# Two layers of block 1: turned dilated heads, weight parts and out weights in another order

## The reference

```python
h = rmsnorm(x, attn_norm[l])
c_q, c_kv, k_r, q_d, k_d, v_d = jnp.split(h @ w_in[l], split_at, axis=-1)
o_a = mla_mixer(c_q, c_kv, k_r, cos, sin, g_cq[l], g_ckv[l], w_uq[l], w_ukv[l], ...)
q_d = rmsnorm(q_d.reshape(B, S, DIL_HEADS, DIL_HD), g_dil_q[l])
k_d = rmsnorm(k_d.reshape(B, S, DIL_HEADS, DIL_HD), g_dil_k[l])
o_b = dilated_attention(q_d, k_d, v_d, rel_bias)
mixed = jnp.concatenate([o_a.reshape(B, S, -1), o_b.reshape(B, S, -1)], axis=-1)
x = x + mixed @ w_out[l]
x = x + conv_ffn(rmsnorm(x, ffn_norm[l]), w_up[l], conv_w[l], conv_b[l], w_down[l])
```

## Time and profile before

| | us |
|---|---|
| median of 3 runs | 1795.7 (1791.6 to 1797.75) |
| profiled execution | 1792.91 |
| its span, first to last instruction | 1791.1 |
| PE busy | 1646.6 |
| DVE busy | 1128.8 |
| ACT busy | 844.1 |
| POOL busy | 263.7 |
| mean granted clock of TensorE | 0.972 |

### The profile page before, as it was taken

How to read it: one execution, slowest core, us unless ns; L and a number is a source line. 1 busy time by engine, 2 the same in 40 slices (tenths; PEclk the granted TensorE clock), 3 DMA queues, 4 the chain that set the end, 5 groups by cost and what they waited for, 6 DMA issues and landing times. The chain is left out here.

```text
span 1791.1 us, 22878 instructions
## 1 busy us (share of the span) xinstructions
PE 1646.6 (92%) x8652; PEld 1323.4 (74%) x8652; DVE 1128.8 (63%) x1881; ACT 844.1 (47%) x1506; POOL 263.7 (15%) x322
## 2 busy tenths in 40 slices
PE   8989999998999999798799899999999696989996
PEld 7667887785687877586557688888787584668875
DVE  5586898466768995625574744444333656579964
ACT  5554776364646664522153633333222532466643
POOL 2000114500021118000000001111630000001171
PEclk9999999999999999999999999999999798989998
DMA  7456765554678545431264533333222341236651
GB/s 258 151 204 178 204 191 172 193 174 151 214 241 215 162 151 186 139 102 47 74 229 122 160 99 94 94 94 96 93 94 95 118 136 47 70 108 188 188 188 47
DMA packets 266496, 258.32 MB, mean 144 GB/s; under 512 B 8822, under 2 KB 208730, under 8 KB 266131
## 3 DMA queue, kind: packets, MB, share of 16 engines
q1 hardware_dynamic: 262706, 245.36, 45.0%
q0 software_dynamic: 3536, 11.42, 1.8%
q10 hardware_dynamic: 144, 0.07, 0.0%
HBM read 255.72 MB, written 1.10 MB: 143 GB/s over the span
## 5 line engine op out<-in xcount | busy, mean ns | idle before, releaser
L551 PE MATMUL psv<-hHL,wH 128*128 128x512 f32 (+1 forms) x1952 | 639.6, 390 | 12.4 <-issue 9.0
L1167 DVE TENSOR_TENSOR wL<-ring,wH 128x1024 fp32r<-128x1024 f32 (+2 forms) x364 | 451.8, 1247 | 296.3 <-ACT wH L1715 293.3
L1715 ACT ACTIVATE wH<-ring 128x1024 fp32r<-128x1024 f32 (+2 forms) x364 | 376.2, 1040 | 311.3 <-PE psv L551 305.4
L551 PE MATMUL psv<-hHL,wL 128*128 128x256 f32 (+1 forms) x1504 | 466.7, 310 | 0.0
L551 PEld LDWEIGHTS psv<-hHL,wH 128*128 128x128 f32 x1952 | 365.0, 189 | 94.9 <-issue 10.5
L551 PE MATMUL psv<-wH,hHL 128*128 128x512 f32 (+2 forms) x936 | 321.3, 392 | 39.7 <-DVE wL L1167 27.5
L551 PEld LDWEIGHTS psv<-hHL,wL 128*128 128x128 f32 x1504 | 285.3, 190 | 15.9
L551 PE MATMUL pss<-wH,hHL 128*128 128x512 f32 (+3 forms) x808 | 274.9, 385 | 0.0
L551 PEld LDWEIGHTS psv<-wH,hHL 128*128 128x128 f32 x936 | 177.2, 190 | 84.6 <-DVE wL L1167 22.6
L551 PE MATMUL psv<-wL,hHL 128*128 128x512 f32 (+2 forms) x468 | 181.4, 388 | 0.0
L551 PEld LDWEIGHTS pss<-wH,hHL 128*128 128x128 f32 x808 | 153.1, 191 | 29.7
(11 more groups left out here) (238 smaller groups left out, 1758.9 us busy)
## 6 DMA issues: line engine op xcount, KB each, us to landing
ring<-in_w_up SPq DMA_DIRECT2D x176, 512.0 KB, 5.2
ring<-in_w_mod SPq DMA_DIRECT2D x96, 512.0 KB, 4.8
ring<-in_w_down SPq DMA_DIRECT2D x88, 512.0 KB, 4.4
ring<-in_w_in SPq DMA_DIRECT2D x52, 512.0 KB, 4.7
ring<-in_w_out SPq DMA_DIRECT2D x32, 512.0 KB, 4.7
ring<-in_w_in SPq DMA_DIRECT2D x8, 384.0 KB, 5.9
ring<-in_w_in SPq DMA_DIRECT2D x8, 288.0 KB, 6.8
ring<-in_w_ukv SPq DMA_DIRECT2D x4, 512.0 KB, 4.3
```

The lines of the kernel that those rows point to most:

```text
L551: return pe.matmul(o, a, b, start=start, stop=stop, skip_group_check=True)
L1167: v.tensor_tensor(lo, raw, hi.bitcast(F32), ALU.subtract).then_inc(piece_split, told("piece_split", p))
L1715: return ac.activation(o, i, ACT.Copy)
```

## The change

- In part 2 of the input projection ACT converts the next weight piece (2.2) before the latent squares instead of behind them, and the roots of the four sums are taken together at the end, two columns at a time (`squares` in place of `sumsq`).
- PE turns the dilated heads behind the lifts, ahead of the bands and of part 4, instead of behind part 4. DVE's and ACT's copies of them move ahead too, DVE's before the sums of the lifted heads, ACT's behind their squares. The squares of the first token tile go to another area of `W`.
- ACT converts piece 4.2 between the lift copies; DVE makes its low part before its copies of the turned heads (4.0 and 4.1 stay where they were). ACT no longer waits for `dil_heads`, and loads the table of the exponential before it copies the dilated values.
- Pieces out 0.0 and out 0.1 are no longer split before the attention: ACT takes out 0.0 in step 8 and out 0.1 behind the attention, DVE takes out 0.0 in step 8 and out 0.1 in step 9, each ahead of that step's other work.
- All modulation chunks of the attention come before the out weights in the order of the chunks.

```diff
-        sqm = [w_at(14464, 16, MQK), view(scr, 0, 16, MQK)]
+        sqm = [w_at(10368, 16, MQK), view(scr, 0, 16, MQK)]
...
-            add_cols(A["w_out"][l], 0, 512, ph, "out", 0, between=lambda: add_mod(0, MOD1[l]["pairs"].values()))
+            add_mod(0, MOD1[l]["pairs"].values())
+            add_cols(A["w_out"][l], 0, 512, ph, "out", 0)
...
+                pe.wait_ge(dil_heads, at("dil_heads", ph))
+                for t in range(NT):
+                    for g in range(2):
+                        transposes("VS"[g], (ph, "dT", t, g),
...
                 if l == 0:
                     pe.wait_ge(table_spread, at("table_spread", "all"))
...
                 project_split(range(NT), [512] * NT, (ph, "in", 4))
-                pe.wait_ge(dil_heads, at("dil_heads", ph))
-                for t in range(NT):
-                    for g in range(2):
-                        transposes("VS"[g], (ph, "dT", t, g),
...
+            def attention(ph, units, l=0, mods={}, heads=None, early=(0, ())):
...
+                    if p in early[1]:
+                        splits_to(early[0], p - early[1][0])
...
+                splits_to(first_piece[ph, "in", 4], 2)
+                for t in range(NT):
+                    v.wait_ge(V_full, at("V_full", ph, "dT", t, 0))
+                    b = bank("V", ph, "dT", t, 0)
+                    v.tensor_scalar(dT[:, 0:4, t * P:(t + 1) * P], b[:, :].rearrange("p (k n) -> p k n", k=4),
+                                         col("g_dil_q", l), None, ALU.mult).then_inc(V_free, told("V_free", ph, "dT", t, 0))
                 for t in range(NT):
                     v.wait_ge(head_squares, at("head_squares", ph, "mla", t))
...
-                splits_to(first_piece[ph, "in", 4], 2)
                 v.wait_ge(head_roots, at("head_roots", ph, "mla"))
...
-                input_rows(4, dvh[:, 0, :, :])
-                for t in range(NT):
-                    v.wait_ge(V_full, at("V_full", ph, "dT", t, 0))
...
-                splits_to(first_piece[ph, "out", 0], 1)
+                v.wait_ge(V_full, at("V_full", ph, "in", 4, 0))
+                v.tensor_copy(dvh[:, 0, :, :], bank("V", ph, "in", 4, 0)[:, :].rearrange("p (h d) -> p h d", h=8)).then_inc(V_free, told("V_free", ph, "in", 4, 0))
...
-                attention(ph, units1, 0, MOD1[l]["pairs"], mla_columns)
+                attention(ph, units1, 0, MOD1[l]["pairs"], mla_columns, (first_piece[ph, "out", 0], (8, 9)))
...
+            def squares(x, n, c, *key):
+
+                ac.wait_ge(sum_of_squares, at("sum_of_squares", *squared[-1]))
+                squared.append(key)
+                ac.activation(junk[:, 0:n], x, ACT.Square, accum_out=ss[:, c:c + 1]).then_inc(sum_of_squares, mark("sum_of_squares", *key))
+                ac.wait_ge(sum_of_squares, at("sum_of_squares", *key))
...
+                splits_to(first_piece[ph, "in", 2])
                 for base, off, n in ((0, 0, QL), (3, QL, KVL)):
                     for t in range(NT):
                         ac.wait_ge(FREE["VS"[t]], at("VS"[t] + "_free", ph, "in", 1 if base else 0, t))
-                        sumsq(lat[:, t, off:off + n], n, 8 + (2 if base else 0) + t, ph, "lat", base, t)
+                        squares(lat[:, t, off:off + n], n, 8 + (2 if base else 0) + t, ph, "lat", base, t)
+                for f, o in ((ACT.Sqrt, root), (ACT.Identity, ss)):
+                    for c, n in ((8, QL), (10, KVL)):
+                        ins = ac.activation(o[:, c:c + 2], ss[:, c:c + 2], f, scale=1.0 / n, bias=eps_col[:, 0:1])
+                ins.then_inc(root_ready, mark("root_ready", ph, "lat", 3, 1))
...
+                splits_to(first_piece[ph, "in", 4], 2)
                 for c in range(2):
                     for t in range(NT):
                         ac.wait_ge(S_full, at("S_full", ph, "lift", 3, c, t))
...
-                ac.wait_ge(dil_heads, at("dil_heads", ph))
...
+                for t in range(NT):
+                    ac.wait_ge(S_full, at("S_full", ph, "dT", t, 1))
+                    b = bank("S", ph, "dT", t, 1)
+                    copy(dT[:, 4:8, t * P:(t + 1) * P], b[:, :].rearrange("p (k n) -> p k n", k=4), col("g_dil_k", l)).then_inc(S_free, mark("S_free", ph, "dT", t, 1))
...
-                input_rows(4, dvh[:, 1, :, :])
...
-                splits_to(first_piece[ph, "out", 0], 1)
+                splits_to(first_piece[ph, "in", 4] + 3, 0)
+                load_table(ACT.Exp)
+                ac.wait_ge(S_full, at("S_full", ph, "in", 4, 1))
+                copy(dvh[:, 1, :, :], bank("S", ph, "in", 4, 1)[:, :].rearrange("p (h d) -> p h d", h=8)).then_inc(S_free, mark("S_free", ph, "in", 4, 1))
...
-                attention(ph, units1, mla_columns)
+                attention(ph, units1, mla_columns, (first_piece[ph, "out", 0], (8,)))
```

More of the change, by code:

```diff
@@ L862, in _ @@
                         owed.append(used)
+                pe.wait_ge(dil_heads, at("dil_heads", ph))
+                for t in range(NT):
+                    for g in range(2):
+                        transposes("VS"[g], (ph, "dT", t, g),
+                                   [(dqk[:, t, 8 * g + 2 * k:8 * g + 2 * k + 2, :].rearrange("p a b -> p (a b)"),
+                                     slice(k * P, k * P + P)) for k in range(4)])
                 if l == 0:
@@ L869, in _ @@
                 project_split(range(NT), [512] * NT, (ph, "in", 4))
-                pe.wait_ge(dil_heads, at("dil_heads", ph))
-                for t in range(NT):
-                    for g in range(2):
-                        transposes("VS"[g], (ph, "dT", t, g),
-                                   [(dqk[:, t, 8 * g + 2 * k:8 * g + 2 * k + 2, :].rearrange("p a b -> p (a b)"),
-                                     slice(k * P, k * P + P)) for k in range(4)])
                 def mla_transposes(t):
@@ L1241, in low_features1 @@
                                         ALU.subtract).then_inc(FREE[kind], told(kind + "_free", ph, "hT", t))
-            def attention(ph, units, l=0, mods={}, heads=None):
+            def attention(ph, units, l=0, mods={}, heads=None, early=(0, ())):
                 n = len(units) // 2
@@ L1519, in _ @@
                 rotate(x1, x2, tab, tmp).then_inc(mla_heads, told("mla_heads", ph))
-                input_rows(4, dvh[:, 0, :, :])
-                for t in range(NT):
-                    v.wait_ge(V_full, at("V_full", ph, "dT", t, 0))
-                    b = bank("V", ph, "dT", t, 0)
-                    v.tensor_scalar(dT[:, 0:4, t * P:(t + 1) * P], b[:, :].rearrange("p (k n) -> p k n", k=4),
-                                         col("g_dil_q", l), None, ALU.mult).then_inc(V_free, told("V_free", ph, "dT", t, 0))
-                splits_to(first_piece[ph, "out", 0], 1)
+                v.wait_ge(V_full, at("V_full", ph, "in", 4, 0))
+                v.tensor_copy(dvh[:, 0, :, :], bank("V", ph, "in", 4, 0)[:, :].rearrange("p (h d) -> p h d", h=8)).then_inc(V_free, told("V_free", ph, "in", 4, 0))
                 def mla_columns(t):
@@ L1798, in to_features, with attention @@
                     copy(hH[:, :, t * P:(t + 1) * P], raw_h[:, t % 2, :, :]).then_inc(feat_high, mark("feat_high", ph, t))
-            def attention(ph, units, heads=None):
+            def attention(ph, units, heads=None, early=(0, ())):
                 n = len(units) // 2
@@ L1953, in _ @@
                 head_root(*(a[:, 32:64].rearrange("p (t h) -> p t h", t=NT) for a in (hroot, hx)), MQK, 8, ph, "mla")
-                input_rows(4, dvh[:, 1, :, :])
-                for t in range(NT):
-                    ac.wait_ge(S_full, at("S_full", ph, "dT", t, 1))
-                    b = bank("S", ph, "dT", t, 1)
-                    copy(dT[:, 4:8, t * P:(t + 1) * P], b[:, :].rearrange("p (k n) -> p k n", k=4), col("g_dil_k", l)).then_inc(S_free, mark("S_free", ph, "dT", t, 1))
-                splits_to(first_piece[ph, "out", 0], 1)
+                splits_to(first_piece[ph, "in", 4] + 3, 0)
+                load_table(ACT.Exp)
+                ac.wait_ge(S_full, at("S_full", ph, "in", 4, 1))
+                copy(dvh[:, 1, :, :], bank("S", ph, "in", 4, 1)[:, :].rearrange("p (h d) -> p h d", h=8)).then_inc(S_free, mark("S_free", ph, "in", 4, 1))
                 def mla_columns(t):
```

## The result

The changed kernel takes 1786.7 us (median of 4 runs, 1785.56 to 1787.0), the kernel before 1796.33 (4 runs, 1791.6 to 1797.75): a ratio of 0.995 with a 95% interval of 0.9931 to 0.9969. The forecast was 1784.0. The profiled execution took 1785.56 us, its span is 1783.7 us, 7.4 less than before.

A forecast was written before the change was run, and what follows sets the result against it. TensorE, busy for 92% of the span, was taken as the bound, so only its idleness could be gained. Gains of 17.1 us less losses of 5.4 gave 11.7 us faster, median 1784.0 us, range 1778 to 1791.

The forecast's parts named there:

- rival (f): Both attention tails: the table switch holds the copy behind it 1.4 us longer, giving 1786.8 us; chance 0.02.
- Part 1: Input projection 2: weight piece 2.2 ahead of the latent squares gains 3.1 us in layer 0, 1.3 in layer 1.
- Part 2: Lifts to first maxima: heads turned before projection 4; with fewer low parts ahead, 5.1 us gained in layer 0, 7.6 in layer 1.
- Rival (a): Attention tail: it costs nothing, so up to 17.1 us gained, span 1778.6; chance 0.14.
- (d): Layer 1: out 0's weights over 0.8 us late hold the last copies, 1786 with 2 us; chance 0.18 with (b), (f).
- the ring: SP's weight queue: modulation chunks ahead of the out weights; out 0 still lands in time, cost 0, bounds 0 and 1.5 us.
- Rival (b): Inside the attention: half the head gain is given back, 5 to 6 us, 1790; chance 0.18 shared with (d), (f).
- Rival (c): Attention's end held by something not starting sooner, such as modulation weights: 1.0 us slower, 1796.7; chance 0.08.
- Part 3: Attention tail: out 0.1 ahead of the last head pair on DVE loses 2.45 us in layer 0, 1.45 in layer 1.
- The half clock of layer 0: Output projection of layer 0: PE's 3.4 us idleness brings slow clock, 1.5 us lost, bounds 0 and 1.7.
- the last term: Layer 1's tail: PE's 1.5 us idleness, near the harmless 1.33, brings no clock loss.
- Rival (e): Half-clock stretches elsewhere shift by chance: 1.5 us each, two more or fewer make 3 us either way; no chance of its own.

The follow-up runs named there:

- e9: Kernel after, with the high part of out 0.1 ahead of ScalarE's square-root table load instead of behind it: 1783.89 us, ratio 0.9935 to before.
- e5: Kernel before, unchanged, profiled a second time: span end 1792.8 us.
- e11: Kernel before, unchanged, profiled a third time: 1791.81 us.
- e4: Kernel before with only the heads turned ahead of projection 4, copies moved and piece 4.2 between lift copies: 1791.81 us, ratio 0.9978.
- e1: Kernel after, with VectorE taking piece out 0.1 behind the attention instead of in step 9: 1780.05 us, ratio 0.9909 to before.
- e10: The kernel of e1, unchanged, profiled again: 1781.87 us.
- e7: Kernel before with only the new chunk order and the late out pieces 0.0 and 0.1: 1797.52 us, ratio 1.0016.
- e6: Kernel after, unchanged, profiled again: span end 1782.2 us.
- e12: The kernel of e3, unchanged, profiled again: span end 1791.3 us.
- e8: Kernel of e1 plus useless matmuls in TensorE's short waits at the attention's end: 1780.73 us, ratio 0.992 to before.
- e3: Kernel before with only piece 2.2 ahead of the latent squares and the roots taken together: 1793.03 us, ratio 0.999.
- e2: Kernel after plus useless matmuls, 28 in layer 0 and 12 in layer 1, before TensorE's wait for the last pair: 1784.97 us, ratio 0.994.

## Why the prediction was right, point by point

The direction, the mechanism and nearly all terms stood; one term was set wrongly, and the forecast came out 2.7 us below the median. That the median, 1786.7, falls on the number of rival (f), 1786.8, is chance: e9 shows that the load has no such cost.

**Part 1.** Forecast 3.1 us in layer 0, measured 2.78. The new wait is before piece 2.3 as said, 1.39 us instead of 1.1, since each square, which now waits for its own end, steps by up to 0.73 us. In layer 1 forecast 1.3; the way from norm 0 to lifts 1 is 240.80 us before, 240.61 and 240.78 in e5 and e11, and 239.14 in after: about 1.6. The forecast took the gain of 3.1 as sure; e11 and e4 show the same wait of 2.6 us without half clock, so 1.0 us of it is clock that some executions of before do not lose. The working that priced a stretch from 41.49 to 45.75 as 4.3 - 2.75 = 1.5 us left out that the next piece would not have been ready: at full clock the way is 3.12 us (e11), so the difference there is 1.1. As a price for the output projection, which has no such wait, 1.5 is close to the 1.37 to 1.66 us measured; that the number fits there is in part luck.

**Part 2.** The transposes have no wait in their new place (72.33, right at the end of the lifts), and TensorE shows no wait for VectorE's L1524 any more. The first maxima of layer 0 come 4.69 us earlier relative to the lifts (forecast 5.1), those of layer 1 7.64 (forecast 7.6). The 0.4 us of layer 0 are the last low part of projection 4: its end, where VectorE starts to scale the heads, lies 27.01 us behind the lifts (84.73) instead of 26.42, 0.59 later where 0.18 was forecast. ScalarE's high part ahead of it waits for TensorE to release a buffer, before and after; TensorE is 0.59 us later at the second piece of projection 4 (24.28 us behind the lifts instead of 23.69), less than the 0.75 forecast, but all of it comes through to the low part. (1.75 less 0.87, which the forecast rounds to 0.75, is 0.88.) For layer 1 VectorE's timeline of after shows where the gain lies:

```profile
427.94 3.35 DVE L1522 TENSOR_TENSOR W<-W,hr 128x3072 f32<-128x3072 f32 x1
...
435.67 0.41 DVE L1261 CUSTOM_DVE_ANT_0 scr<-psv,W 128x256 f32<-128x256 f32 x1
```

It is 7.73 us from the one to the other, where 435.37 to 448.65 was 13.28: 5.55 of the 7.64. The other 2.09 lie ahead of it, the inverse that starts earlier. The cost of 0 for converting piece 4.2 between the lift copies held by its second reason and not its first: it did wait for its weights, 1.24 us in layer 0 and 1.38 in layer 1, and ScalarE caught up. ScalarE's timeline of after, layer 0:

```profile
67.39 1.06 ACT L1718 ACTIVATE wH<-ring 128x1024 fp32r<-128x1024 f32 x1 [1.24 <-DMA ring<-in_w_in]
```

**Rival (a)** fell with the tail's cost, and **(d)** with the ring below. **Rival (b)** fell: the attention moves whole. With the tail's piece away it takes 45.60 and 45.03 us (e1, e10) against 45.03 before, 46.01 against 46.03 in layer 1. **Rival (c)** fell with it: nothing held the attention's end.

**Part 3.** Forecast 2.45 us in layer 0, measured 47.45 - 45.03 = 2.42; forecast 1.45 in layer 1, measured 1.42. e1 shows the cause by its removal, e7 by itself. The half clock of layer 0 was put at 1.5 us and cost 1.37 (1.59 in e6).

**The step that was mis-sized** is the last term: "In layer 1 the idleness is 1.5 us, near the harmless 1.33", taken as 0. Behind those 1.45 us the profiled execution ran at 0.55 to 0.60 and its output projection took 1.62 us more; e6 took none, after the same 1.45 us, and e7 took it again (25.68 us). The right term is a chance of 1.6 us, not 0. With it the sum is 10.1 where the profile shows 9.94 behind the changed part; e6, without it, shows 11.83, where 11.7 were forecast. That close a fit owes something to the execution counted from: against e11 the two show 8.11 and 10.00.

**The ring.** Its cost was 0 as taken: ScalarE waited 0.24 us for out 0.0's weights in layer 1, and the high part was there in time. ScalarE's timeline of after, layer 1:

```profile
475.88 1.06 ACT L1718 ACTIVATE wH<-ring 128x1024 fp32r<-128x1024 f32 x1 [0.24 <-DMA ring<-in_w_out]
```

**Rival (f)** fell with e9. **Rival (e)**, the clock by chance, is what is left of the error: on the way from norm 1 to the end, code that no version changes takes 1272.4, 1274.2 and 1273.1 us before, 1274.9 and 1275.3 in after, 1277.6 and 1278.5 in e1 and e10. The forecast's sentence that everything behind hangs on PE and moves with it did not hold: of the 9.94 us at norm 1 the span kept 7.4. Much of it goes with the clock. Added up over this part, the stretches with a granted clock of 0.50 come to 75.5, 85.7 and 79.0 us before, 85.8 and 95.9 in after, and 95.9 in both e1 and e10; one such stretch follows a wait of 1.75 us in after (at 540.96), while behind the same wait in before, 1.76 us at 550.61, there is none. It is not all: e12 and e8 have 96.0 us each and take 1275.2 and 1278.5. Why the later part should draw more half clock in the changed kernels stays open; it was not tried apart.

**Why the parts don't add up.** The ratios of the three parts alone are 0.999, 0.9978 and 1.0016, together 0.16% faster or 2.9 us; the whole is 0.5% faster, 9.0 us. Measured at norm 1 instead, in the table, the parts give -1.42 (-2.68 in e12), -6.0 and +1.52, together -5.9 to -7.2, and after shows -9.94 and -11.83. Two things fill a good part of that: part 1 alone keeps 2.68 of some 4.6 us in e12 and gives the rest back, 0.7 of it to half clock in the scores behind the wait for the turned heads, a wait that part 2 removes, and in e4 a half clock of 1.6 us fell on an output projection that in e5 and before had none. The medians add the untouched part, which in e3, e12 and e4 took 1275.2 to 1278.1 us against 1272.4 to 1274.2 before. The rest is not settled.

## What to carry to other kernels

Before work is put into a gap of an in-order engine, follow its own input: if that comes later than the last thing which a busier engine needs from the same queue, the whole chain behind it moves; here one piece of weights ahead of the last head pair cost 3.8 us and the clock behind it, and taking one number out of a tuple brought a further 7 us. Count such a piece as moved past everything that stands behind it, as the prediction did, and then try the version without it. A gain of few microseconds that hangs on the clock is to be read at points of the profile and in several executions, not in one span.

## What the runs showed of the hardware

- The half clock (granted 0.50, 1.2 instead of 2.4 GHz) does not follow from the length of the wait alone. Behind 2.61 us in projection 2 it came in before, e5 and e7 (granted 0.50, 0.50 and 0.51 from 42 to 44 us) and not in e11 and e4 (1.00); behind 1.45 us ahead of the output projection in after and e7 and not in e6; behind 0.98 us in e3 and e4 and not in before or, with 0.99, in e12. Behind about 3.4 us (after, e6, e7) and 1.90 us (e9) it came each time. It cost 1.4 to 1.7 us each time on an output projection of 24.05 to 24.10 us. The Trainium skill (TensorE: Matmul & The Clock Gate, What's actually happening, the note on the warm-up budget) says that the number of slow matmuls at a kernel's start varies from run to run; in the middle of this kernel the traces agree, and go further: whether there are any varies too.
- A stretch at half clock halves the rate and not more: of matmuls of 512 columns one starts 0.42 us behind the other instead of 0.23 (TensorE's timeline of before, below). Short waits of 1 to 1.5 us can so cost more by their clock than by themselves: 0.98 us of wait and 1.6 us of clock in e3.

```profile
42.09 0.63 PE L551 MATMUL psv<-wL,hHL 128*128 128x512 f32 x1
...
42.51 1.05 PE L551 MATMUL psv<-wH,hHL 128*128 128x512 f32 x2
...
45.99 0.39 PE L551 MATMUL psv<-wL,hHL 128*128 128x512 f32 x1
...
46.22 0.63 PE L551 MATMUL psv<-wH,hHL 128*128 128x512 f32 x2
```

- Matmuls without a use in a wait kept the clock at 1.00 (e2, layer 0: 24.10 instead of 25.44 us) and cost nothing where they ended as TensorE was released (e2, both layers). Half clock also came inside the attention of layer 1, away from the tail: it went with 49.0 us (e2) and 48.06 (e9) from maxima to projection, where after and e6 at full clock took 47.45.
